# Six two-head units a layer for the block-sparse attention of a decoder trunk, in place of sixteen one-head steps

## The reference

```python
def hybrid_layer(x, norm_w, w_in, w_out, ...):
    h = rmsnorm(x, norm_w)
    proj = h @ w_in                                  # 512 x 4160
    y_rwkv = rwkv7_time_mix(...) * silu(...)
    y_conv = short_conv_mix(...) * silu(...)
    y_moba = moba_attention(q, k, v, rel_bias) * silu(...)
    y_ret = retention_chunkwise(...) * silu(...)
    return x + jnp.concatenate([y_rwkv, y_conv, y_moba, y_ret], axis=-1) @ w_out

# moba_attention, for each head and each block of 128 queries; with 512 positions and
# blocks of 256 keys, every earlier block is selected, so it is causal attention
s = einsum('hqd,hkd->hqk', q * Dh ** -0.5, k) + bias[q_pos - k_pos]   # masked where k_pos > q_pos
prob = softmax(s, axis=-1)
y = einsum('hqk,hkd->hqd', prob, v)
```

## Time and profile before

| | before |
|---|---|
| median of three runs | 733.91 us (732.66 to 734.82) |
| the profiled execution, first to last instruction | 732.6 us |
| PE busy | 699.9 us (96%) |
| DVE busy | 396.0 us (54%) |
| POOL busy | 415.2 us (57%) |
| ACT busy | 188.9 us (26%) |
| mean granted TensorE clock | 0.985 of full |

### The profile page before, as it was taken

The page is one execution under the profiler, slowest core; times in us unless marked ns, Lnnn a source line. Parts: engine busy times, 40 slices in busy tenths (PEclk is TensorE's granted clock), DMA queues, the critical chain, the costliest instruction groups (busy, mean ns, idle before and its releaser), DMA issues.

```text
span 732.6 us, 11998 instructions
## 1 busy us (share of the span) xinstructions
PE 699.9 (96%) x4955; PEld 532.3 (73%) x4955; DVE 396.0 (54%) x607; ACT 188.9 (26%) x357; POOL 415.2 (57%) x334
## 2 busy tenths in 40 slices
PE   4999999999999999979999999999999999996995
PEld 3778778777776766758887777887787676664784
DVE  5868854601166455773354886280115643679433
ACT  4352012211332225321133311121124222423111
POOL 4698986442442344559929899653442424228860
PEclk9999999999999999989999999999999999998998
DMA  8758344172212111244433323417222111006502
GB/s 266 222 158 207 81 116 94 15 173 59 59 30 59 30 52 36 58 128 131 158 100 87 87 64 87 107 44 154 59 58 59 38 50 30 1 26 190 157 1 115
DMA packets 122615, 66.83 MB, mean 91 GB/s; under 512 B 31359, under 2 KB 115907, under 8 KB 122435
## 3 DMA queue, kind: packets, MB, share of 16 engines
q1 hardware_dynamic: 122562, 66.08, 33.3%
HBM read 55.85 MB, written 10.22 MB: 90 GB/s over the span
## 4 chain that ended last, share of the span: by engine, by line
PE 90%; DVE 6%; DMA 1%; ACT 1%; issue 1%; SPq 0%; DVEq 0%; ACTq 0%
PE bank L634 22%; PE bank L636 20%; PE bank L635 19%; PE bank L813 3%; PE bank L797 3%; PE bank L779 3%; PE bank L805 2%; PE bank L732 2%; DVE act_lo L1584 2%; PE bank L936 1%; DMA pages<-in_x_dram 1%; PE bank L946 1%; PE bank L938 1%; PE bank L838 1%; PE bank L785 1%; DVE x_or_y L1446 1%
## 5 line engine op out<-in xcount | busy, mean ns | idle before, releaser
L559 POOL TENSOR_TENSOR w_hi<-w_raw,constants 128x512 fp32r<-128x512 f32 x164 | 184.7, 1147 | 293.5 <-PE bank L636 231.4
L634 PE MATMUL bank<-act_hi,w_hi 128*128 128x512 f32 x656 | 274.4, 418 | 12.1 <-DVE act_lo L1584 7.8
L635 PE MATMUL bank<-act_hi,w_lo 128*128 128x512 f32 x656 | 258.5, 394 | 0.0
L636 PE MATMUL bank<-act_lo,w_hi 128*128 128x512 f32 x656 | 258.4, 394 | 0.0
L566 POOL TENSOR_TENSOR w_lo<-w_raw,w_hi 128x512 fp32r<-128x512 f32 x164 | 233.3, 1443 | 0.0
L634 PEld LDWEIGHTS bank<-act_hi,w_hi 128*128 128x128 f32 x656 | 124.1, 189 | 63.2 <-issue 25.3
L636 PEld LDWEIGHTS bank<-act_lo,w_hi 128*128 128x128 f32 x656 | 124.4, 190 | 27.4
L635 PEld LDWEIGHTS bank<-act_hi,w_lo 128*128 128x128 f32 x656 | 124.7, 190 | 23.6 <-issue 1.9
L1089 ACT ACTIVATE pages<-bank 128x512 f32<-128x512 f32 x24 | 14.3, 598 | 119.9 <-PE bank L636 119.9
L1595 DVE TENSOR_TENSOR x_or_y<-x_or_y,bank 128x512 f32<-128x512 f32 x16 | 11.0, 688 | 49.8 <-PE bank L636 49.8
L1432 DVE SCALAR_TENSOR_TENSOR pages<-bank,bias 128x128 f32<-128x128 f32 (+3 forms) x32 | 15.7, 492 | 40.5 <-PE bank L813 40.4
(11 more groups left out here) (176 smaller groups left out, 849.7 us busy)
## 6 DMA issues: line engine op xcount, KB each, us to landing
w_raw<-in_w_in_dram SPq DMA_DIRECT2D x66, 512.0 KB, 4.2
w_raw<-in_w_out_dram SPq DMA_DIRECT2D x16, 512.0 KB, 4.2
x_scratch<-x_or_y SPq DMA_DIRECT2D x16, 256.0 KB, 4.6
x_or_y<-x_scratch SPq DMA_DIRECT2D x16, 256.0 KB, 3.6
pages<-in_x_dram SPq DMA_DIRECT2D x4, 512.0 KB, 8.7
out_dram<-pages SPq DMA_DIRECT2D x4, 512.0 KB, 3.9
bias_scratch<-pages SPq DMA_DIRECT2D x1, 1280.0 KB, 7.6
constants<-in_consts_dram SPq DMA_DIRECT2D x1, 1128.5 KB, 6.7
```

What stands on the lines that cost most here:

```text
L559: pool.tensor_tensor(w_hi[:, i % HI, k, :], raw, const("one").unsqueeze(2).to_broadcast([P, H, P]), ALU.mult).then_inc(s("w_high"), 1)
L634: mm(b[:, :], hi, act_hi[:, k, :], start=n == 0, stop=False)
L635: mm(b[:, :], lo, act_hi[:, k, :], start=False, stop=False)
L636: ins = mm(b[:, :], hi, act_lo[:, k, :], start=False, stop=n == KT - 1)
```

## The change

`PARTS` cuts the four query blocks into (0, 1), (2) and (3); a unit is one part for both heads of a pair, so there are six units a layer: widths 128 + 256, then 384, then 512, for the first pair and again for the second. `attend` becomes four steps:

- `attend_scores(u)` after slot 11 + 2u: PE computes the scores of both heads, the matmul of one head following that of the other, the first head's on array rows 0 to 63 into bank 2, the second's on rows 64 to 127 into bank 3. DVE adds the bias and takes the maxima, ACT exponentiates.
- `attend_norm(u)` in the middle of slot 12 + 2u: DVE scales by the reciprocal sums, for one head and then the other.
- `attend_turn(u)` in the middle of slot 13 + 2u, as the last step ahead of a quarter of a projection: PE transposes the first head's probabilities into bank 2, then the second's into bank 3; ACT copies both out.
- `attend_values(u)` after slot 13 + 2u, ahead of the scores of unit u+1: PE multiplies by the values, the two heads in turn, on array columns 0 to 63 and 64 to 127. `attend_out` follows units 2 and 5.

The last scores thus come after slot 21 (before: 26) and the last values after slot 23 (before: 28).

```diff
+PARTS = ((0, 1), (2,), (3,))
+UNITS = 2 * len(PARTS)
...
-    for g in range(18):
-        after[11 + g].append(("attend", g))
-        if g in (9, 17):
-            after[11 + g].append(("attend_out", g // 10))
+    for u in range(UNITS + 1):
...
+        if u > 0:
+            mid[11 + 2 * u].append(("attend_turn", u - 1))
+            after[11 + 2 * u].append(("attend_values", u - 1))
+            if u % 3 == 0:
+                after[11 + 2 * u].append(("attend_out", u // 3 - 1))
+        if u < UNITS:
+            after[11 + 2 * u].append(("attend_scores", u))
+            mid[12 + 2 * u].append(("attend_norm", u))
...
+                    for qb, c0, w in unit_blocks(u):
+                        last = qb == PARTS[u % len(PARTS)][-1]
+                        for hh in range(2):
+                            hr = head_rows(hh)
+                            ins = mm(banks[hh][:, c0:c0 + w], MQ[hr, p, qb * P:(qb + 1) * P], MK[hr, p, 0:w], start=True, stop=True)
...
+                def attend_turn(u):
+                    first, n = unit_first(u), len(unit_blocks(u))
+                    for hh in range(2):
+                        pe.wait_ge(*at("prob_norm", layer, first + (hh + 1) * n))
+                        b = begin(f"pt{u}_{hh}", layer)
+                        for _, c0, w in unit_blocks(u):
+                            for c in range(c0, c0 + w, P):
+                                ins = pe.transpose(b[:, c:c + P], PB[:, hh, c:c + P], ident)
+                        end(ins, f"pt{u}_{hh}", layer)
...
+                            for hh in range(2):
+                                h = 2 * p + hh
+                                ins = mm(yb[head_rows(hh), qb * P:(qb + 1) * P], rows["mv"][:, kb, h * N:(h + 1) * N],
+                                         PT[:, hh, c0 + kb * P:c0 + (kb + 1) * P], start=kb == 0, stop=kb == qb)
```

More of the change, by code:

```diff
@@ L86, with unit_blocks, unit_first @@
 N_CONST = _at
+PARTS = ((0, 1), (2,), (3,))
+UNITS = 2 * len(PARTS)
+def unit_blocks(u):
+    out, at = [], 0
+    for qb in PARTS[u % len(PARTS)]:
+        out.append((qb, at, (qb + 1) * P))
+        at += (qb + 1) * P
+    return out
+def unit_first(u):
+    return sum(2 * len(PARTS[v % len(PARTS)]) for v in range(u))
 def layer_steps():
@@ new lines, in attend_scores @@
+                def attend_scores(u):
+                    p = u // len(PARTS)
+                    if u == 0:
+                        for j in ("mq0", "mq1", "mk0", "mk1"):
+                            pe.wait_ge(*read(j, layer))
+                    banks = [begin(f"s{u}_{hh}", layer) for hh in range(2)]
+                    for qb, c0, w in unit_blocks(u):
[3 more added lines that the diff above has]
+                            ins = mm(banks[hh][:, c0:c0 + w], MQ[hr, p, qb * P:(qb + 1) * P], MK[hr, p, 0:w], start=True, stop=True)
+                            if last:
+                                end(ins, f"s{u}_{hh}", layer)
@@ new lines, in attend_norm @@
+                def attend_norm(u):
+                    e, n_q = unit_first(u), len(unit_blocks(u))
+                    for hh in range(2):
+                        e += n_q
+                        dve.wait_ge(*at("prob", layer, e))
+                        link(dve.reciprocal(row_scale[:, 2 * hh:2 * hh + n_q], row_sum[:, 2 * hh:2 * hh + n_q]))
+                        for j, (_, c0, w) in enumerate(unit_blocks(u)):
+                            pb, n = PB[:, hh, c0:c0 + w], 2 * hh + j
+                            ts(pb, pb, row_scale[:, n:n + 1], None, ALU.mult).then_inc(s("prob_norm"), 1)
```

115 lines of the change are left out of this document (51 added, 64 removed).

## The result

The changed kernel takes 701.6 us (median, 698.66 to 702.66) where the kernel before took 733.61 us beside it on the same chip: a ratio of 0.9552, 95% interval 0.9526 to 0.9577 (the two medians alone would give 0.9564). The prediction was 702.7 us with a range of 696 to 712. The profiled execution has a span of 698.8 us; that of before had 732.6.

What follows compares the result with a forecast made beforehand. PE bounds the kernel, its time in attention steps lying on the path. 16.6 us saved less 2.0 waits a layer (29.2 for both) plus 2.0 at the second end takes 732.6 to 701.4 span, 702.7 median; range 696 to 712.

Steps and rivals of the forecast that it cites:

- PE's cost of a layer, 16.4 us: PE's attention steps and transposes in a layer: 16.4 us instead of 33.0, 16.6 less.
- All four terms: PE's attention work per layer: fewer passages 3.5 us, transposes beside a projection 4.2, scores 4.3, values 4.4.
- The passage straight from values to scores: PE's switch between tilings inside a step: not in the trace, others cost 0.10 to 0.20; five leave 0.5 us doubt a layer.
- Twice the rate on both kinds of halves: Scores on row halves 4.3 us a layer instead of 8.6, values on column halves 4.4 instead of 8.8.
- The two far ends: Other ends of the halves' estimates per layer: scores without overlap 8.6 us, values at L920's share of serial price 7.2.
- Transposes 0.10 each: Transposes beside a projection: 0.10 us each with no fixed cost, 4.2 us for forty in a layer.
- New waits, 2.0 us a layer: PE waiting at transposes for DVE's lumped softmax, and for ACT in slot 23: 2.0 us a layer (0.5 to 6).
- The rival of late lumps: DVE's scalings meet POOL more often, each unit waits about 1 us longer: 6 to 8 us, 709; chance 0.11.
- The second layer end, 2.0 us: Second layer's end: w_out weights load earlier, POOL no longer idles, 16.3 us becomes 14.3 like the first, saving 2.0.
- The first layer end, nothing: First layer's tail starts when PE gets there, moves with PE and gives nothing back; DVE arrives in time.
- the rival "the end takes it back": DVE's reciprocals and finishes run late in shorter slots, each layer end loses 2 to 3 us: 708; chance 0.06.
- The rival "slower": Scaled probabilities over 2.9 us late at each of 12 units lose; at 4 us a unit 747 us; chance 0.04.

Runs made afterwards that it cites:

- the first experiment: The kernel before, still sixteen one-head units, with only the transposes moved to the middle of slot 13 + h, beside a projection: 743.65 us, ratio 1.0126 to before.

## Why the prediction came out right, and where it did not

**PE's cost of a layer, 16.4 us: 16.3 measured.** All four terms hold. The signs that were named for it came too: pairs start together, four blocks of values for both heads take 1.03 us, a unit of values and scores adds 1.85 to 2.08, and the clock row has a 9 in every slice of the attention slots. The passage straight from values to scores, which no row of before showed, costs what the others do: the step of 1.85 us leaves 0.01 us over the sum.

**Twice the rate on both kinds of halves: right.** The two far ends (8.6 for scores, 7.2 for values) were given up for the nearest rows, and the runs show why that was right for the values: L920, which first does one half and then the other, is the order of the run head by head, not the changed kernel's. The Trainium skill's rule (TensorE: Matmul & The Clock Gate, "The mechanism"), that a weight load overlaps only matmuls on another group of rows, would forbid this if taken alone, and does not show here: all values use all rows, and in alternation they run at twice the rate. (The same section also lets a load into the background weight buffer go ahead.) Nor do two halves stay at the 77% of full use that its "Measured speedup vs the span model" has for four row tiles: pairs of row halves lose nothing.

**Transposes 0.10 each: right** (4.1 us for 40).

**New waits, 2.0 us a layer: wrong, they are none.** The step that failed is the price of the scaling. It put 1.25 us on each 384-wide scaling, the mean of the earlier trace rows, and so unit 1 came out 0.6 to 1 us late. In the changed kernel the same operation reads, by form and then in the timeline around unit 1 with POOL's pieces:

```profile
L1488 DVE TENSOR_SCALAR pages<-pages,small 128x384 f32<-128x384 f32 x8 | 3.6, 450 | 0.3
...
217.62 2.54 POOL L589 TENSOR_TENSOR w_lo<-w_raw,w_hi 128x512 fp32r<-128x512 f32 x2
...
222.59 0.42 DVE L1488 TENSOR_SCALAR pages<-pages,small 128x384 f32<-128x384 f32 x1
```

Before, the scaling at 219.20 (1.15 us) met POOL's w_lo, which ran from 217.61 for 2.52 us, and so did the other three 384-wide scalings of that layer. Now POOL is done at 220.16 and idle until 226.45; three of the four scalings lie in such gaps and take 0.42 us; the fourth touches the end of one and takes 0.54. Two of them 0.8 us shorter are 1.6 us, and the second head's scaling is done at 223.0, 1 us ahead of the transposes at 224.05. The Trainium skill (SBUF — State Buffer, "SBUF: two separate sides") says that VectorE, in a 2-port mode or with two inputs in SBUF, and GpSimd take turns at one pair of ports, and that the loser waits out the other's whole instruction. The trace agrees in kind: 0.73 us were added at 219.20, beside a w_lo piece of 2.52 / 2 = 1.26 us that had some 0.9 us to go. The mean was sound as a mean and no price for another place. The rival of late lumps asked this very question from the other side; the other 384-wide operations, 0.55 for a maximum, were the row to take. In slot 23 the copies of ACT end at 273.03 and the values start at 273.27, so there too the wait was just missed. What such waits would have cost, the run with the scaling one slot later shows: 16 us, their length and time at the lower clock level.

**The second layer end, 2.0 us: 0.8 measured.** The mechanism was there (POOL no longer idles for w_out), the size was not. The step took the first end as the pattern and the difference of 16.3 and 14.3 us as the price of the transfer. The runs show another price: taken back alone, the earlier load costs 3.5 us. With it the end is 15.5 us and without it 19.0. What the load sets is which steps of DVE lie beside POOL's, and that also depends on everything else that had moved. That the second end becomes like the first was right for the wait (7.54 and 7.29 us from start to start); the 14.3 us that were expected of both had no term for how long PE then stays at the lower clock level, 5.2 us here and 2.7 there.

**The first layer end, nothing: 0.1 measured, in part by luck.** The prediction had the tail move with PE. But PE's idle time before it grew from 5.40 us to 6.91, so DVE arrives later than PE by 1.5 us more, which is what the rival "the end takes it back" says. It does not show in the sum, because behind it 6 matmuls instead of 12 ran at the lower clock level. In the other traces with the same end the sum is 0.2 to 1.1 us longer than before.

**Two misses that partly cancelled.** 4.0 us of waits that did not come, and 1.2 us of layer end that stayed, make 2.8 us in favour; the span was predicted at 701.4 and is 698.8, 2.6 less. In the median 1.1 us are left (702.7 to 701.6), which is inside the spread of the runs. That the total lies so near is luck to that extent; PE's cost is not.

**The rival "slower"** needed each of twelve units more than 2.9 us late. The run with the scaling late is the worst case of that mechanism that was tried; it costs up to 3.5 us at a unit with the clock behind it, but 1.4 to 1.7 at most of the others and nothing at two in six, and the kernel stays 2% faster than before (0.977 to 0.982). The other way of losing was not among the rivals, and is the one that the first experiment met: ACT's queue. With one slot to a unit the copy of the transposes stood behind `ln_square`. The changed kernel has its transposes in the odd slots 13 to 23, so none meets `ln_square` in slot 22 or `ln_scale` in slots 27 and 28.

## What to carry to other kernels

Price a step that moves by its duration in the cover of its new place: the same VectorE operation took 0.42 us between GpSimd's pieces and 1.15 beside them. When PE work is to be shortened by putting two heads side by side, alternate them matmul by matmul; head after head gives back about half of it. A wait of PE can cost more than it lasts: at unit 0 of the run with the scaling late, 1.5 us of idle time and the lower clock behind it made 3.5. And where a layer's end waits for the low parts of a split, do all products with the high parts first: that was worth 11 us here, after moving the same waiting work earlier had brought 5.

## What the runs showed of the hardware

- Two fp32 matmuls of 128 columns on the two column halves with all rows in use (128*64) run side by side when alternated: 1.03 us for 2 x 4 blocks, as long as 4 blocks alone. In the order head by head about 0.4 us of overlap is won whatever the length (1.51 us for the same 8).
- DVE's scaling and act_lo subtraction, both from and to SBUF, slow down beside POOL's splitting, and POOL's beside them. The scaling of 384 took 0.42 us or 1.15 to 1.52. Five act_lo subtractions took 4.16 us or 8.02 us; POOL's pair of w_hi takes 2.04 us alone and 2.93 beside them. The maximum and bias steps of the softmax kept their times in both kernels (0.55 us for 384), beside POOL or not.
- After PE had idled 7 us, its matmuls lay 0.43 us apart, the lower clock level, for 5.2 us (638.86 to 644.10) at one end and 2.7 us (303.25 to 305.95) at the other, with almost the same wait before. After an idle time of 2.50 us within an attention slot it was slow as well (2.07 us for scores that took 1.05), and after 1.50 us twice; after 1.44 us once and once not; after 1.10 and 1.25 us not. In the kernel with the high parts first, which has no such idle time at the layer ends, the clock stays at its full level there.
